# A decoder block on one core: a third bank for attention scores, one bank for turned probabilities

## The reference, cut to what matters

```python
def block(args):                        # differential attention, 4 heads, a block of 128 queries
    s = einsum('bhiqd,bhikd->bhiqk', q_blk, k) * scale + bias
    p = softmax(where(dist >= 0, s, NEG))
    a = p[:, :, 0] - lam * p[:, :, 1]   # two maps, the second subtracted
    return einsum('bhqk,bhkv->bhqv', a, v)
...
# sparse attention, 8 heads: three results, weighted by gates
o = gates[..., 0:1] * o_cmp + gates[..., 1:2] * o_slc + gates[..., 2:3] * o_win
...
x = x + concatenate([o_diff, o_nsa]) @ w_out
h = rms_norm(x, norm2)
x = x + (silu(h @ w_gate) * (h @ w_up)) @ w_down
```

## Time and profile before

| What | Before |
|---|---|
| median of 3 runs | 651.25 us (651.13 to 651.65) |
| profiled execution, its own time | 652.01 us |
| its span, first to last instruction | 650.2 us |
| PE busy | 638.5 us (98%) |
| DVE busy | 452.8 us (70%) |
| ACT busy | 354.5 us (55%) |
| GpSimd (POOL) busy | 245.5 us (38%) |
| chain that ended last | PE 95%, DVE 2%, DMA 1%, POOL 1% |

### The profile page before, as it was taken

One profiled execution on the slowest core, in us unless ns is written; L12 is line 12 of the kernel. 1 busy time (PEld: TensorE's weight loads), 2 busy tenths in 40 slices (PEclk: granted clock), 3 DMA queues, 4 the chain that ended last, 5 costly groups with the idle time before them and its releaser, 6 DMA issues.

```text
span 650.2 us, 11350 instructions
## 1 busy us (share of the span) xinstructions
PE 638.5 (98%) x4029; PEld 571.1 (88%) x4029; DVE 452.8 (70%) x957; ACT 354.5 (55%) x697; POOL 245.5 (38%) x152
## 2 busy tenths in 40 slices
PE   8999999999999999999999999999999999999996
PEld 7888998988899887888888899999999998888884
DVE  5435437655656887634279898888988898788984
ACT  7646435879565568625332464444454456655653
POOL 4766344575161542453302103435353320121521
PEclk9999999999999999999999999999999999999999
DMA  8979979479997998997399957878777668989813
GB/s 245 274 177 232 256 201 230 109 196 329 278 233 174 228 203 217 188 229 206 111 305 283 257 162 245 256 231 253 219 241 216 198 219 318 318 243 257 291 64 129
DMA packets 116007, 146.58 MB, mean 225 GB/s; under 512 B 5252, under 2 KB 73968, under 8 KB 115952
## 3 DMA queue, kind: packets, MB, share of 16 engines
q1 hardware_dynamic: 96936, 110.49, 53.9%
q0 software_dynamic: 16352, 30.84, 27.2%
q10 hardware_dynamic: 2664, 4.53, 2.0%
HBM read 139.53 MB, written 59.00 MB: 305 GB/s over the span
## 4 chain that ended last, share of the span: by engine, by line
PE 95%; DVE 2%; DMA 1%; issue 1%; POOL 1%; ACT 0%; DVEq 0%; ACTq 0%; POOLq 0%
PE bank L821 10%; PE bank L823 10%; PE bank L822 10%; PE bank L1161 8%; PE bank L1159 8%; PE bank L1160 8%; PE bank L840 7%; PE bank L842 7%; PE bank L841 7%; PE bank L1001 6%; PE bank L977 3%; PE bank L961 3%; PE bank L962 2%; PE bank L1040 1%; DMA rows<-in_cmp_pos_v_dram 1%
## 5 line engine op out<-in xcount | busy, mean ns | idle before, releaser
L766 POOL TENSOR_TENSOR w_lo<-raw,w_hi 128x1024 fp32r<-128x1024 f32 (+1 forms) x63 | 156.9, 2493 | 225.6 <-ACT w_hi L1202 224.7
L1202 ACT CAST w_hi<-raw 128x1024 fp32r<-128x1024 f32 (+2 forms) x123 | 127.1, 1039 | 123.2 <-PE bank L1161 44.9
L1676 DVE CUSTOM_DVE_ANT_0 bank<-bank,bias 128x128 f32<-128x128 f32 (+3 forms) x96 | 47.6, 497 | 75.8 <-PE bank L962 40.0
L1833 DVE TENSOR_TENSOR w_lo<-raw,w_hi 128x1024 fp32r<-128x1024 f32 (+1 forms) x61 | 72.9, 1195 | 12.9 <-ACT w_hi L1202 12.9
L840 PE MATMUL bank<-xT_hi,w_hi 128*128 128x512 f32 x200 | 79.9, 399 | 0.0
L842 PE MATMUL bank<-xT_hi,w_lo 128*128 128x512 f32 x200 | 78.7, 394 | 0.0
L841 PE MATMUL bank<-xT_lo,w_hi 128*128 128x512 f32 x200 | 78.6, 393 | 0.0
L1159 PE MATMUL bank<-xs,w_hi 128*128 128x256 f32 x256 | 72.3, 282 | 0.0
L1161 PE MATMUL bank<-xs,w_lo 128*128 128x256 f32 x256 | 72.2, 282 | 0.0
L1160 PE MATMUL bank<-xs,w_hi 128*128 128x256 f32 x256 | 72.2, 282 | 0.0
L787 POOL DMA_DIRECT2D down_sums<-in_w_down_dram x21 | 23.3, 1111 | 109.6 <-DMA down_sums<-in_w_down_dram 54.9
(11 more groups left out here) (287 smaller groups left out, 1703.8 us busy)
## 6 DMA issues: line engine op xcount, KB each, us to landing
raw<-mixed_sums SPq DMA_DIRECT2D x32, 512.0 KB, 4.8
raw<-in_w_gate_dram SPq DMA_DIRECT2D x22, 512.0 KB, 4.8
raw<-in_w_in_dram SPq DMA_DIRECT2D x20, 512.0 KB, 5.5
down_sums<-in_w_down_dram POOLq DMA_DIRECT2D x17, 512.0 KB, 8.7
mixed_sums<-in_w_up_dram SPq DMA_DIRECT2D x16, 512.0 KB, 10.8
mixed_sums<-in_w_gate_dram SPq DMA_DIRECT2D x16, 512.0 KB, 9.1
mixed_sums<-mixed_sums POOLq DMA_DIRECT2D x16, 512.0 KB, 12.6
raw<-in_w_up_dram SPq DMA_DIRECT2D x14, 512.0 KB, 4.8
```

The lines of the kernel that those rows point to most:

```text
L766: nc.gpsimd.tensor_tensor(wv_lo(k)[:, 0:n], raw_at(k)[:, 0:n], wv_hi(k)[:, 0:n].bitcast(F32), ALU.subtract).then_inc(s_split, 1)
L1202: nc.scalar.copy(wv_hi(k)[:, 0:n], raw_at(k)[:, 0:n]).then_inc(s_whi, 1)
L1833: nc.vector.tensor_tensor(wv_lo(k)[:, 0:n], raw_at(k)[:, 0:n], wv_hi(k)[:, 0:n].bitcast(F32), ALU.subtract).then_inc(s_dlo, 1)
```

## The change

The eight banks of the attention are shared out anew: three banks for scores, used in turn (`s % 3`), and one bank for all turned probabilities. The waits follow: `scores(s)` waits for the exp (or combination) of slot s-3, and `turn_probs` of turn n for the copy of turn n-1. Nothing else of the program is touched: the two halves of `PT`, the four slots of `E`, `STEP_PIECES` and the order of every engine stay.

```diff
-        PROJ, SCORE, TURN, OUTP = ps[0:2], ps[2:4], ps[4:6], ps[6:8]
+        PROJ, SCORE, TURN, OUTP = ps[0:2], ps[2:5], ps[5], ps[6:8]
...
             def scores(s):
                 kind, h, b, i = slots[s]
-                bank = SCORE[s % 2]
+                bank = SCORE[s % 3]
...
-                if s >= 2 and slots[s - 2][0] == "diff" and slots[s - 2][2] == 1:
-                    pe.wait_ge(s_comb, sum(1 for z in slots[:s - 1] if z[0] == "diff" and z[2] == 1))
-                elif s >= 2:
-                    pe.wait_ge(s_exp, s - 1)
+                if s >= 3 and slots[s - 3][0] == "diff" and slots[s - 3][2] == 1:
+                    pe.wait_ge(s_comb, sum(1 for z in slots[:s - 2] if z[0] == "diff" and z[2] == 1))
+                elif s >= 3:
+                    pe.wait_ge(s_exp, s - 2)
...
             def turn_probs(s):
...
-                if n >= 2:
-                    pe.wait_ge(s_pt, n - 1)
+                if n >= 1:
+                    pe.wait_ge(s_pt, n)
                 for j in range(2 if kind == "cmp" else i + 1):
-                    mm = nc.tensor.transpose(TURN[n % 2][:, j * P:(j + 1) * P], E[:, s % E_SLOTS, j * P:(j + 1) * P],
+                    mm = nc.tensor.transpose(TURN[:, j * P:(j + 1) * P], E[:, s % E_SLOTS, j * P:(j + 1) * P],
                                              ident[:, :])
...
-                nc.scalar.copy(PT[:, n % 2, 0:w], TURN[n % 2][:, 0:w]).then_inc(s_pt, 1)
+                nc.scalar.copy(PT[:, n % 2, 0:w], TURN[:, 0:w]).then_inc(s_pt, 1)
```

More of the change, by code:

```diff
@@ L1279, in exps @@
                 if kind == "cmp":
-                    nc.scalar.activation(E[:, s % E_SLOTS, 0:n], SCORE[s % 2][:, 0:n], ACT.Exp, scale=-1.0).then_inc(s_exp, 1)
+                    nc.scalar.activation(E[:, s % E_SLOTS, 0:n], SCORE[s % 3][:, 0:n], ACT.Exp, scale=-1.0).then_inc(s_exp, 1)
                 else:
-                    to = SCORE[s % 2] if kind == "diff" and b == 1 else E[:, s % E_SLOTS, :]
-                    nc.scalar.activation(to[:, 0:n], SCORE[s % 2][:, 0:n], ACT.Exp, scale=-1.0,
+                    to = SCORE[s % 3] if kind == "diff" and b == 1 else E[:, s % E_SLOTS, :]
+                    nc.scalar.activation(to[:, 0:n], SCORE[s % 3][:, 0:n], ACT.Exp, scale=-1.0,
                                          bias=nmax[:, s % 8:s % 8 + 1], accum_out=total).then_inc(s_exp, 1)
@@ L1705, in weigh @@
                     n = (i + 1) * P
-                    e0, e1 = E[:, (s - 1) % E_SLOTS, 0:n], SCORE[s % 2][:, 0:n]
+                    e0, e1 = E[:, (s - 1) % E_SLOTS, 0:n], SCORE[s % 3][:, 0:n]
                     link(nc.vector.reciprocal(ssum[:, s:s + 1], ssum[:, s:s + 1]))
```

## The result

| What | Before | After |
|---|---|---|
| median of 4 runs each, same chip | 651.23 us | 664.29 us (662.77 to 666.92) |
| ratio, with its 95% interval | | 1.0204 (1.0171 to 1.0236) |
| profiled execution, its own time | 652.01 us | 664.40 us |
| its span | 650.2 us | 662.6 us |

Slower by 13.1 us, near the forecast and inside the range. As the rest shows, two errors of the sum offset each other. The page of the changed kernel first: span, busy time of two engines, and the granted clock in 40 slices of the span.

What follows compares the result with a forecast made beforehand. PE's in-order queue was taken as the bound. Nine late-copy holds of 13.7 us less 2.4 of saved waits gave +11.3: 663.3 us for the profiled execution, 662.6 for the median, range 657.0 to 668.5.

Steps and rivals of the forecast that it cites:

- Bound and sign: Whole kernel: PE's queue is the bound, holds in the attention come out at the end; slower, chance 0.88.
- Held once: Rival, attention: one hold sets PE back for good, every later copy is early; +0.2, 651.4 us, chance 0.07.
- Every copy bare: Rival, attention: turn and copy alternate strictly, all 84 copies fall on PE; +33.0, 684.3 us, chance 0.04.
- The scores count: Rival, attention: the turns' waits shrink to nothing, the gain at the score matmuls remains; 649.75 us, chance 0.05.
- the 1.5 that the sum took whole: Score matmuls (L961): three waits for the combined difference map, 1.5 us, all counted as gain of the third score bank.
- The term of 2.57: Turn at 73.46 us: would wait 2.57 us for the preceding copy, run at 75.57 behind a weight cast.
- 0.76 off for the execution: Whole kernel: the median of the runs lay 0.76 us below the profiled execution, so 663.3 became 662.6.
- The term of 2.40: Turn at 143.65 us: would wait 2.40 us for the preceding copy, which ran at 145.59.
- Between groups a held PE does not get ahead of anything: Attention: DVE and ACT follow PE and move back with it, so the late groups add, to 13.7 us.
- the other seven terms: Turns at 114.47, 125.74, 151.82, 209.10, 225.67, 236.25, 241.00 us: holds of 0.74, 1.33, 1.77, 1.80, 1.14, 0.85, 1.14 us.
- places that were left out or counted within a group: Attention turns: three single places of 0.16 to 0.33 us omitted; eleven beside the nine, 5.2 us, not added.
- The 0.9 us of L1001's "issue": Value matmuls (L1001): two waits for turned copies, 0.9 us, would go, being spent in the turn ahead.

Runs made afterwards that it cites:

- the single hold of turn 60: Kernel before, with turn 60 (at 209.10 us) alone waiting for the copy just before it, all banks as before: 653.65 us, ratio 1.0034.
- the kernel with the holds filled: Changed kernel with 30 idle matmuls ahead of eight of the waiting turns, so that PE is busy while held: 660.25 us, ratio 1.0137.
- turn 10 alone: Kernel before, with turn 10 (at 73.46 us) alone waiting for the copy of turn 9: 650.96 us, ratio 1.001.
- the run with this hold alone: Kernel before, with turn 33 (at 143.65 us) alone waiting for the copy of turn 32: 653.79 us, ratio 1.0042.
- the reorderings: Changed kernel: weight casts behind next copy 660.45 us, copies one step earlier 657.44, turn behind projection pieces 660.92. Kernel before with the casts moved: 653.17.
- the turn behind the pieces: Changed kernel with PE's step reordered to scores, pieces of projection, turn, values: 660.92 us, ratio 1.0141.

## Why the prediction was right, and where it was wrong

**Bound and sign: right.** PE is the bound, what holds it in the attention comes out at the end, and the stretch behind swallows nothing (369.00 before and after). With one turned bank alone the time is the same within the spread; the single hold of turn 60 stayed on PE to the end (1.84, forecast 1.80). "Held once", which needs later copies to be early after a first hold, is refuted by that and by the eight jumps of the table. "Every copy bare" would have needed +33.0; 10 of 83 turns waited. "The scores count" fell too, though on less: in the changed kernel the waits at L961 went as forecast. The setback shrinks at their three places by 0.35 (160.56 before), 0.60 (213.13) and 1.06 (248.89), but the value product right behind the last then waits for DVE and gives 0.80 back: some 1.2 net. In the kernel with the holds filled, where no slow clock covers it, the next value product waits behind the second place too, for 0.47, and some 0.7 is left of the 1.5 that the sum took whole.

**The term of 2.57: wrong.** The late cast at 74.62 was that execution's chance. It is also why that execution lay above its median: the profiles of the runs with turn 10 alone and turn 60 alone, the same up to there but without the late cast, are 0.9 and 1.1 us ahead of it by 114.47. I took 0.76 off for the execution and yet kept in the sum a term that was part of the same chance.

**The term of 2.40: wrong, with the step behind it.** "Between groups a held PE does not get ahead of anything" failed here. The copy was to move back with PE. PE was set back 1.22 ahead of this group, but the copy moved only from 145.59 to 145.85. Two casts ahead of it had waited for transfers in the kernel before:

```profile
139.30 1.05 ACT L1202 CAST w_hi<-raw 128x1024 fp32r<-128x1024 f32 x1 [0.33 <-DMA raw<-in_cmp_w_v_dram]
...
144.64 1.05 ACT L1202 CAST w_hi<-raw 128x1024 fp32r<-128x1024 f32 x1 [0.38 <-DMA raw<-in_w_in_dram]
```

In the changed kernel the same two casts and the copy behind them stand as

```profile
140.09 1.03 ACT L1202 CAST w_hi<-raw 128x1024 fp32r<-128x1024 f32 x1
...
144.92 1.06 ACT L1202 CAST w_hi<-raw 128x1024 fp32r<-128x1024 f32 x1
145.85 0.40 ACT L1295 COPY PT<-bank 128x256 f32<-128x256 f32 x1
```

The exp ahead of the first cast moved by 1.21 (138.41 to 139.62), with PE; the first cast moved by 0.79 and the second by 0.28. Each had a wait for a transfer, and that wait took up a part of PE's setback before the rest could reach the copy. Of 2.40 there remained 0.97 here and 0.52 at the turn ahead. The waits for PE of the earlier trace rows were totals over the whole attention; where casts wait for transfers and ACT is otherwise full (9.36 of 10.78 us in the run with this hold alone) the copy follows only in part. Elsewhere the step held, the other seven terms being off by 0.01 to 0.19.

**The clock: not priced.** The prediction named a fall of the clock only as what would make it wrong. It fell for 10.24 us right behind the hold of 1.44, and PE's setback grew by 4.2 in that time; against the filled run the cost is 3.9. The same matmuls kept PE busy for 236.24 us in the attention, where the prediction had it stay near 231. The Trainium skill, "TensorE: Matmul & The Clock Gate", section "A second HAM failure mode: psum-queue depth-cycling", tells of a kernel in which short idle times between groups of matmuls, from cycling through PSUM banks, made the clock swing between its two levels, at a loss of throughput. This trace agrees in part: the clock fell behind a wait for a PSUM bank, to 0.50 for 10.24 us, where the kernel before has 1.00 in the whole attention; but it fell once, and behind nine of the ten holds, one of 1.58 us among them, it did not.

**The sum.** Forecast +11.3 of holds less gains against some 9 measured (660.25 - 651.35 = 8.9 with the holds filled), and 0 of clock against some 4. Of the places that were left out or counted within a group, two held PE, each with a jump of 0.52: 162.41 before, and 142.33, the turn ahead named above. The holds were too much by about 2.4 and the clock too little by about 4: the total is near by cancellation. The forecast that L977 would wait for 10 to 20 us missed with 9.0, and holds of 2 to 3 us occurred nowhere. The 0.9 us of L1001's "issue" went as forecast, but one of the two was itself the chance cast's.

## What to carry to other kernels

Before a buffer is taken from a pair, lay the end of each release beside the start of the use that would now wait for it, over the whole trace: 73 of 83 turns show no wait here, and one place alone, held, cost 1.7 us for good. Check first whether a large term is one execution's chance (a row that waits for a DMA), and whether the engine that is late also waits for the one it holds in that very stretch, with no wait for a transfer in between; only then do holds add in full. Where TensorE is the bound, price a hold twice, as the time it lasts and as what the clock may do behind it (here some 9 and some 4 us); and moving the late work only pays if nothing else needs the place it moves to, as the reorderings here showed.

## What the runs showed of the hardware

- Behind single holds of 1.44, 1.78 and 1.79 us, with PE busy 8.96 of 10.45, 7.19 of 8.97 and 8.99 of 10.78 us ahead, the granted clock fell to 0.50 for 10.24, 3.41 and 3.41 us; with one turned bank and two score banks it fell for 10.24 and 3.41 us behind 1.45 and 1.03, and with the turn behind the pieces for 3.41 behind three shorter holds (0.44, 0.18 and 0.75). It did not fall behind a hold of 1.58 us in the changed kernel, nor behind one of 1.67 in the profiled execution with one hold. It fell in some executions of the same program and, by the mean clock, not in others (0.999 against 0.992 to 0.997 with one hold). Which activity decides is not settled by these runs; with the holds filled by idle matmuls no such stretch occurs in the attention of the profiled execution.
- A combination on DVE with both inputs in SBUF took 1.66 us while POOL ran a subtraction of two SBUF tiles, and ended 0.16 after it (213.40 for 213.24); with one input in a bank it took 0.35 beside the same subtraction. The Trainium skill, "GPSIMD Engine Reference", section "Specifications", says that GpSimd's way into SBUF is shared with VectorE and that DVE instructions with two SBUF inputs contend for it. The trace agrees, with the numbers above.
